# Attention over 416 of 512 key columns, with tokens kept by grid columns from the second norm to the output

## The reference

```python
h = _rmsnorm(x, pre_g[i]) * (1.0 + sc[:, None, :]) + sh[:, None, :]
hc = _rmsnorm(ctx, pre_g[i]) * (1.0 + sc_c) + sh_c
parts = _split_in(h @ w_in[i])
q = _apply_rope(_heads(parts[4]), cos, sin)
k = _apply_rope(_heads(parts[5]), cos, sin)
...
attn = _neighbourhood_attention(q, k, v, k_c, v_c, rpb[i])
y = _mixer_out(parts, attn, conv_w[i], conv_b[i], w_out_conv[i], w_out_attn[i], w_o[i])
...
x = x + gt[:, None, :] * _rmsnorm(y, post_g[i])
```

## Time and profile before

| | |
|---|---|
| time, 3 runs | 1209.0, 1209.19, 1211.04 us; median 1209.19 |
| profiled execution, its own time | 1211.35 us |
| its span | 1209.5 us |
| granted TensorE clock, mean | 0.991 |
| busy: PE, PEld | 1158.9 us (96%), 682.9 us (56%) |
| busy: DVE, ACT, POOL | 492.9, 239.3, 107.0 us |
| moved by DMA | 324.58 MB, mean 268 GB/s |

### The profile page before, as it was taken

One profiled execution on the slowest core, in us unless ns is written; L12 is line 12 of the kernel. 1 busy time (PEld: TensorE's weight loads), 2 busy tenths in 40 slices (PEclk: granted clock), 3 DMA queues, 4 the chain that ended last, 5 costly groups with the idle time before them and its releaser, 6 DMA issues.

```text
span 1209.5 us, 13265 instructions
## 1 busy us (share of the span) xinstructions
PE 1158.9 (96%) x5276; PEld 682.9 (56%) x5276; DVE 492.9 (41%) x832; ACT 239.3 (20%) x452; POOL 107.0 (9%) x116
## 2 busy tenths in 40 slices
PE   6999999999999999999989898899999999999997
PEld 6887888888344454453433243454447854456643
DVE  2146348424111201111111111276755676577677
ACT  2232554202100000000000000111001011038811
POOL 0016135000000000000000000000000020025300
PEclk9999999999999999999999999999999999999999
DMA  9999323377799999999999999954546446443300
GB/s 319 344 289 331 127 71 104 105 287 312 310 422 412 407 413 414 414 414 421 414 422 421 422 421 422 347 207 140 173 139 203 146 144 218 142 166 128 102 6 35
DMA packets 118999, 324.58 MB, mean 268 GB/s; under 512 B 8736, under 2 KB 66208, under 8 KB 94368
## 3 DMA queue, kind: packets, MB, share of 16 engines
q1 hardware_dynamic: 113200, 316.32, 68.9%
q0 software_dynamic: 1536, 4.20, 1.1%
q10 hardware_dynamic: 4208, 3.31, 0.9%
HBM read 322.75 MB, written 1.05 MB: 268 GB/s over the span
## 4 chain that ended last, share of the span: by engine, by line
PE 85%; DMA 9%; DVE 2%; ACT 1%; issue 1%; POOL 1%; SPq 0%; DVEq 0%; POOLq 0%
PE bank L719 21%; PE bank L698 17%; PE bank L1025 16%; DMA AR<-in_w 9%; PE bank L701 7%; PE bank L1066 7%; PE bank L1001 2%; PE bank L1037 2%; PE bank L1040 2%; PE bank L1173 1%; PE bank L1206 1%; PE bank L1186 1%; PE bank L1104 1%; PE bank L811 1%; PE bank L1052 1%
## 5 line engine op out<-in xcount | busy, mean ns | idle before, releaser
L698 PE MATMUL bank<-HT,ring 128*128 128x256 f32 x864 | 193.5, 382 | 0.0
L1025 PE MATMUL bank<-ring,AR 128*64 128x512 f32 x608 | 172.6, 610 | 16.0 <-DMA AR<-in_w 10.7
L698 PEld LDWEIGHTS bank<-HT,ring 128*128 128x128 f32 x864 | 163.2, 191 | 27.4 <-issue 6.5
L1025 PE MATMUL bank<-AR 128*64 128x512 f32 x416 | 125.8, 605 | 2.7 <-DMA AR<-in_w 2.6
L2117 DVE TENSOR_TENSOR AR<-AR,bank 128x256 f32<-128x256 f32 x32 | 13.5, 421 | 273.8 <-ACT AR L1427 273.1
L1025 PEld LDWEIGHTS bank<-ring,AR 128*64 128x64 f32 x608 | 50.5, 139 | 106.7 <-issue 103.7
L719 PE MATMUL bank<-ring,AR 128*128 128x512 f32 x224 | 99.8, 604 | 2.1 <-DVE AR L1778 1.1
L719 PE MATMUL bank<-ring,HN 128*128 128x512 f32 x224 | 97.3, 592 | 0.0
L1066 PE MATMUL bank<-ring,AR 128*64 128x512 f32 x352 | 79.6, 594 | 0.0
L719 PEld LDWEIGHTS bank<-ring,AR 128*128 128x128 f32 x224 | 42.8, 194 | 56.0 <-issue 54.0
L719 PE MATMUL bank<-ring,HT 128*128 128x512 f32 x168 | 73.7, 593 | 0.0
(11 more groups left out here) (353 smaller groups left out, 1376.6 us busy)
## 6 DMA issues: line engine op xcount, KB each, us to landing
ring<-in_w SPq DMA_DIRECT2D x120, 1024.0 KB, 17.2
AR<-in_w SPq DMA_DIRECT2D x72, 1024.0 KB, 15.0
ring<-in_w_in SPq DMA_DIRECT2D x61, 1024.0 KB, 7.0
ring<-in_w_mod SPq DMA_DIRECT2D x12, 1024.0 KB, 9.0
AR<-in_w_in SPq DMA_DIRECT2D x6, 1024.0 KB, 18.1
ring<-in_w_out SPq DMA_DIRECT2D x4, 1024.0 KB, 5.4
ring<-in_w_ple_gate SPq DMA_DIRECT2D x4, 1024.0 KB, 9.3
AR<-in_bias POOLq DMA_DIRECT2D x32, 128.0 KB, 2.4
```

Of the source, the lines that this page charges most:

```text
L698: mm = pe.matmul(bank[:, part * T:part * T + T], w[:, k, c0 + part * P:c0 + part * P + P], act[:, k, :], start=(k == 0), stop=(k == k_n - 1))
L1025: mm = pe.matmul(bank[e * SLOT:e * SLOT + SLOT, :].rearrange("p (w n) -> p w n", w=2), XG[:, k, :], w, start=(k == 0), stop=(k == DK - 1))
```

## The change

The tokens behind the second norm are kept in another order: groups of 8 grid columns, all 4 rows of such a group together, so 32 tokens to a group, and tile 0 of the queries holds columns 0 to 31, tile 1 columns 32 to 63. The keys in `KK` lie as tile 0 (128), context (256), tile 1 (128). A window of 16 columns from tile 0 reaches no further than column 39, so tile 0 meets the first 416 entries and tile 1 the last 416 (`met(t)`). Scores, maximum, exponential and scaling run over 416; the other 96 weights are zeroed once on DVE, and turns and values stay at their size.

To get into this order `HT` is written permuted. The convolution needs row order: the turns of `conv` write their bank permuted back, and the last step of `conv_chunk` returns to the new order. ACT moves the context's keys from `KC` into `KK` in five copies. The bias table is permuted on the host, each bias tile is written in two pieces of 128 columns, and the window mask becomes 512 columns wide, so the constants grow by 256 columns. SP copies the input rows from X to `XC` in the new order, in 32 transfers of 8 partitions (32 KB each) inside the core, and stores each half of the output with four transfers of 32 partitions (64 KB) in place of one.

```diff
+BY_COLUMNS = np.arange(T).reshape(T // GW, GW // 8, 8).transpose(1, 0, 2).reshape(-1)
+NEAR = P + 32
...
-                  ("winmask", 256), ("invfreq", 16), ("iota_slot", 128), ("rev8", 8), ("pick2", 2), ("row0", 128), ("round_id", ROUNDS)):
+                  ("winmask", 2 * T), ("invfreq", 16), ("iota_slot", 128), ("rev8", 8), ("pick2", 2), ("row0", 128), ("round_id", ROUNDS)):
...
-        KK = area(1024, 2, DK, T)
-        KT2 = KK[:, 1]
+        KK = area(1024, DK, 2 * T)
+        KT2 = KK.rearrange("p k (b q) -> p k b q", b=4)[:, :, 0:4:3, :]
+        SHK = area(21520, 2, 512)
...
+        XC = area(E0 + 8192, TT, D)
...
+        def met(t):
+
+            return slice(t * (T - NEAR), t * (T - NEAR) + T + NEAR)
...
+        def grid_rows(v):
+
+            return v.rearrange("p (g r c) -> p r g c", r=T // GW, c=8)
...
+            sp.wait_ge(S("na_nmax"), H2 * TT)
+            for g in range(GW // 8):
+                for r in range(T // GW):
+                    n, m = g * 32 + r * 8, r * GW + g * 8
+                    sp.dma_start(XC[n % P:n % P + 8, n // P, :], X[m % P:m % P + 8, m // P, :]).then_inc(S("xrow_in"), 16)
+            rows = out[0].rearrange("(r g c) d -> g r c d", r=T // GW, c=8)
...
-                    sp.dma_start(out[0, t * P:t * P + P, c], HN[:, t, c]).then_inc(S("stored"), 16)
-            sp.wait_ge(S("stored"), 16 * TT * 2)
+                    for g in range(4):
+                        sp.dma_start(rows[4 * t + g, :, :, c], HN[32 * g:32 * g + 32, t, c]).then_inc(S("stored"), 16)
+            sp.wait_ge(S("stored"), 16 * TT * 2 * 4)
...
+                        dst = dst.rearrange("p (r g c) -> p g r c", r=T // GW, c=8)
...
-                    pe.matmul(B[2 + 2 * (u % 2) + e][:, :].rearrange("p (s t) -> p s t", s=2),
-                              QT2[p0:p0 + HD, c, t * P:t * P + P], KK[p0:p0 + HD, :, c, :], start=True, stop=True)\
-                      .then_inc(S("na_s"), 1)
+                    pe.matmul(B[2 + 2 * (u % 2) + e][:, met(t)], QT2[p0:p0 + HD, c, t * P:t * P + P],
+                              KK[p0:p0 + HD, c, met(t)], start=True, stop=True).then_inc(S("na_s"), 1)
...
-                nc.scalar.activation(HT[:, k, :], B[4 + k // 2][:, (k % 2) * T:(k % 2) * T + T], ACT.Identity,
+                nc.scalar.activation(grid_rows(HT[:, k, :]), B[4 + k // 2][:, (k % 2) * T:(k % 2) * T + T]
+                                     .rearrange("p (r g c) -> p r g c", r=T // GW, c=8), ACT.Identity,
...
+            for c0, n in ((4, 4), (2, 2), (1, 1)):
+                if c0 < 4:
+                    act.wait_ge(S("cT"), DK + 3 - c0)
+                nc.scalar.activation(KK[:, c0:c0 + n, P:P + T], KC[:, c0:c0 + n, :], ACT.Copy).then_inc(S("cT"), 1)
+            nc.scalar.activation(YA[:, 0, :], KC[:, 0, :], ACT.Copy).then_inc(S("cT"), 1)
+            act.wait_ge(S("cT"), DK + 4)
+            nc.scalar.activation(KK[:, 0, P:P + T], YA[:, 0, :], ACT.Copy).then_inc(S("cT"), 1)
...
+                pr = PR2[:, n % 4, met(n // 2 % 2)]
+                nc.scalar.activation(pr, pr, ACT.Exp, scale=-1.0, bias=NMX2[:, n % 4:n % 4 + 1],
...
-                        V_.tensor_scalar(HT[:, k, :], src, gain(k), bias(k), ALU.mult, ALU.add).then_inc(S(done), 1)
+                        V_.tensor_scalar(grid_rows(HT[:, k, :]), src.rearrange("p (r g c) -> p r g c", r=T // GW, c=8), gain(k),
+                                         bias(k), ALU.mult, ALU.add).then_inc(S(done), 1)
...
+                m = met(n // 2 % 2)
+                V_.tensor_tensor_reduce(PR2[:, n % 4, m], B[2 + n % 4][:, m], BM[:, n % 4, m], -1.0, 3e38,
...
+                    V_.memset(PR2[:, 0:2, T + NEAR:2 * T], 0.0)
+                    V_.memset(PR2[:, 2:4, 0:T - NEAR], 0.0)
                     na_max(0)
...
+                dve.wait_ge(S("xrow_in"), 16 * (1 + T // 8))
+                V_.scalar_tensor_tensor(out=HN[:, t, c], in0=YF[:, t, c], scalar=rs["y"][:, t:t + 1], in1=XC[:, t, c],
```

More of the change, by code:

```diff
@@ L82, in constants @@
     inv = 10000.0 ** (-np.arange(0, half, 2, dtype=np.float32) / np.float32(half))
-    t = np.arange(T)
+    t = BY_COLUMNS
     d = np.arange(P) % HD
@@ L89, in constants @@
     put("sinT", np.sin(ang.astype(np.float64)) * np.where(i % 32 < 16, -1.0, 1.0)[:, None])
[L90 to L94, removed]
+    col = BY_COLUMNS % GW
+    for tile in range(2):
+        qc, kc = col[tile * P:tile * P + P], col
+        start = np.clip(qc - WIN // 2, 0, GW - WIN)
+        inside = (kc[None, :] >= start[:, None]) & (kc[None, :] < start[:, None] + WIN)
+        at = CONST_COLS["winmask"][0] + tile * T
+        c[:, at:at + T] = np.where(inside, 0.0, -1e30)
     put("invfreq", 10000.0 ** (-np.arange(16, dtype=np.float32) / np.float32(16)))
@@ L1139, in turn_quarter @@
                 for k in range(4):
-                    mm = pe.transpose(TURN_BANKS[name][n][:, k * P:k * P + P], quarter_rows(name, n)[:, k * P:k * P + P], ident)
+                    dst = TURN_BANKS[name][n][:, k * P:k * P + P]
+                    if name == "conv":
+                        dst = dst.rearrange("p (r g c) -> p g r c", r=T // GW, c=8)
+                    mm = pe.transpose(dst, quarter_rows(name, n)[:, k * P:k * P + P], ident)
                 mm.then_inc(S("mT_ps"), 1)
@@ L1182, in values2 @@
                 for kt in range(4):
-                    v = VC if kt < 2 else V2
+                    v = (V2[:, 0], VC[:, 0], VC[:, 1], V2[:, 1])[kt]
                     for e in range(2):
                         h = 2 * c + e
-                        mm = pe.matmul(B[0][e * HD:e * HD + HD, 0:T], v[:, kt % 2, h * HD:h * HD + HD],
+                        mm = pe.matmul(B[0][e * HD:e * HD + HD, 0:T], v[:, h * HD:h * HD + HD],
                                        turned2(c, e)[:, kt, :], start=(kt == 0), stop=(kt == 3))
@@ L1491, in rows_turned @@
                 t, half, _ = QUARTERS[n]
-                dst = {"gated": YA, "conv": UC[:, :, 1:T + 1], "merged": MT}[name]
+                dst = {"gated": YA, "conv": UC[:, :, 1:T + 1], "merged": MT}[name][:, 4 * half:4 * half + 4, :]
                 act.wait_ge(S("mT_ps"), quarter_count(name, n))
-                nc.scalar.activation(dst[:, 4 * half:4 * half + 4, t * P:t * P + P],
-                                     TURN_BANKS[name][n][:, :].rearrange("p (k q) -> p k q", k=4), ACT.Copy)\
-                  .then_inc(S("mT"), 1)
+                if name != "conv":
+                    dst, src = dst[:, :, t * P:t * P + P], TURN_BANKS[name][n][:, :].rearrange("p (k q) -> p k q", k=4)
+                else:
+                    dst = dst.rearrange("p k (r t q) -> p k r t q", r=T // GW, t=TT)[:, :, :, t, :]
+                    src = TURN_BANKS[name][n][:, :].rearrange("p (k r q) -> p k r q", k=4, r=T // GW)
+                nc.scalar.activation(dst, src, ACT.Copy).then_inc(S("mT"), 1)
             first_copy("za")
@@ L1684, in _ @@
                 pool.wait_ge(S(f"bt{n % 4}"), 16 * (n // 4 + 1))
-                bm = BM[:, n % 4, T:2 * T]
-                nc.gpsimd.tensor_tensor(bm, bm, const("winmask"), ALU.add).then_inc(S("bm"), 1)
+                mask = const("winmask").rearrange("p (t b k) -> p t b k", t=TT, b=2)[:, n // 2 % 2]
+                nc.gpsimd.tensor_tensor(bias_at(n), bias_at(n), mask, ALU.add).then_inc(S("bm"), 1)
                 if n >= 2 and n + 2 < H2 * TT:
@@ L2214, in conv_chunk @@
                                              op0=ALU.mult, op1=ALU.add))
-                return V_.tensor_tensor(YA[:, k, :], YA[:, k, :], cv, ALU.mult)
+                ya = grid_rows(YA[:, k, :])
+                return V_.tensor_tensor(ya, ya, cv.rearrange("p (r g c) -> p r g c", r=T // GW, c=8), ALU.mult)
             for m in range(8):
-                s = 1.0 if m >= 4 else HD ** -0.5
-                dst = two(QT2 if m < 4 else KT2, m % 4)
+                s = HD ** -0.5
+                dst = two(QT2, m) if m < 4 else SHK[:, m % 2, :]
                 i = (of["q2"] + of["k2"])[m]
```

22 lines of the change are left out of this document (13 added, 9 removed).

## The result

The changed kernel takes 1213.88 us (median of 6 runs, 1212.19 to 1215.34) beside 1209.39 us for the kernel before (6 runs, 1208.03 to 1211.62). The ratio is 1.0029, 95% interval 1.0019 to 1.0039: slower, by 3.5 us of 1209 (2.3 to 4.7). The forecast was +2.6 us. The change does both of the things that the prediction weighed, a gain in the attention and a loss at the stores.

What follows compares the result with a forecast made beforehand. TensorE, busy 1158.9 of 1209.5 us, bounds the kernel until its end, which hangs on the last store. Scores -2.4, exponential -0.2, stores +5.2 make +2.6 on 1209.19: 1211.8 us, own range 1210.2 to 1212.7, wide range 1207.4 to 1213.6.

Steps and rivals of the forecast that it cites:

- The scores: Attention's score steps on TensorE: 416 columns for 512 save 0.16 us a step, 2.4 us over 15 steps (1.8 to 3.0).
- The constant part of a step: In a score step's 1.06 us on TensorE, 0.20 us does not go with the columns and 0.86 does.
- rival 4: Attention's odd steps: waits for ACT lose half of the 2.4 us, with four store engines 1213.0 us; 0.14 together with rival 3.
- The slack of about 0.3 us in the odd steps: Second head's turns need a bank that ACT empties: 0.36 us to spare, 0.29 left after the change.
- The stores: Kernel's end: sixteen transfers in line on the same four engines, 0.68 us each, 10.9 us; 5.2 us more (4.4 to 5.5).
- the term for an issue: SP's queue at the end: 0.33 us an issue, 0.38 us from one to the next.
- Rival 1: SP's queue at the end: stores spread over all sixteen engines, end costs 1.4 us, 1208.0 us in all; chance 0.22.
- What was taken at nothing: Row copies, ACT's key copies, permuted `HT` writes, conv's turns, longer constants, smaller bias transfers, DVE's fillings: counted as 0 us.
- the cover: Input-row copies on SP: in by about 1160 us, DVE first needs them at 1201.24; holds up to 1.7 us a copy.
- rival 3: Turns of conv on TensorE: they double, +1.75 us, with four store engines 1213.6 us; chance 0.14 together with rival 4.

Runs made afterwards that it cites:

- the four shapes: The kernel before, each output half stored in four transfers, of 2 by 16, 4 by 8, 8 by 4, 16 by 2 rows: 1215.02 us, one time.

## Why the prediction came out right, and where it was off

**The scores.** Forecast 0.16 us a step, 2.4 in all, and 0.2 for ACT's exponential: measured 0.16 a step, 0.08 for the exponential in the chain, and 2.55 together. The constant part of a step that the working assumed fits: without it the step would have lost 0.20. The kernel with 512 keys in the new layout shows the same from the other side: its middle is 2.56 us longer, and its ratio 0.17% higher (2.1 us) than the changed kernel's.

**No wait for ACT in its place** (rival 4). The slack of about 0.3 us in the odd steps held: the turns there went from 1.02 to 1.03 us, and no piece on ACT came into the chain in between.

**The stores.** Forecast 5.2 us (4.4 to 5.5): measured 5.45 in the two profiles, 5.6 between the ratios. The mechanism forecast, four engines and the same four each time, is what the packets, the share of 0.26 and the run with two queues show. But two steps of the working failed. First, the reason I gave from the row, that an engine gets eight rows whatever the size, is wrong: in the kernel before with 32-row stores an engine gets two rows, and only the rule on the slowest dimension, which I had set beside it, fits all of these kernels. By my reason stores of 32 plain rows would have cost 5 us as well; measured, they cost 2.1. Second, the term for an issue, 0.33 us and 0.38 from one to the next, was mis-sized: it is 0.616 and 0.66, nearly the 0.68 I took for moving 64 KB. With a single queue the issues keep almost the pace of the transfers, so the forecast's size was right for one of two limits that nearly coincide, and that they coincide was not foreseen. The run with two queues shows that the four engines alone hold the end at this length. That the issues alone would hold it within about 0.5 us is the estimate under the four shapes.

**Rival 1's price** was mis-sized by the same term. Spread over sixteen engines, stores of 32 plain rows cost 2.1 us and not 1.4, with issues of 0.42 us, one every 0.46. For the stores of the change, whose issues take 0.62, rival 1 would have come out near the forecast itself and not at 1208.0 us. The time alone could then not have told the two apart; the tiny packets, the share of 0.26 and the second queue do.

**What was taken at nothing.** The 32 copies took 21.5 us of SP and not 12, at 0.62 us an issue; they were in by about 1164 and DVE first wanted them at 1196.68, so the cover held. DVE's four writes of `HT` in runs of eight took 1.90 us, not the 2.9 that the working allowed for. The strided writes of `HT`, the turns of conv (rival 3), ACT's copies and the cut bias transfers together cost TensorE 377.88 - 377.88 = 0.00 us behind the norm. The longer constants lie in front of it, and the ratio of the kernel with 512 keys is the best witness for them: 5.6 us (4.1 to 7.1) against 5.4 for its end. That leaves no sign of a price, but would not show one of 0.4 us.

**The number.** 1211.8 us was 1209.19 + 2.6. The ratio applied to the same 1209.19 gives 1212.7, 0.9 above the forecast and inside the range. (The forecast's own range began at 1210.2; its terms, 0.63 us a transfer and 0.20 a step, add up to 1210.4.) The median of the changed kernel's six runs, 1213.88, stands 0.3 above the top of the range. Of the 0.9, 0.25 is the end; the rest is within the ratio's interval (1211.5 to 1213.9).

## What to carry to other kernels

Before splitting or permuting a transfer, look at the slowest dimension of each side: in all kernels here it set how many DMA engines carried it, and the tiny packets in the DMA view count them. Look at the number and the length of the issues beside it, since either can be the limit. A reordering of data is worth choosing by the transfer it ends in: two orders with the same 416 keys differed by 5.2 us in the traces (0.57% between the ratios), because one ends in sixteen stores of 4 by 8 rows and the other in four of 32 by 4. And where a saving sits in the middle of a kernel, time the stretch to the end of the last product and the tail behind it apart; the scatter of everything ahead of them hides both.

## What the runs showed of the hardware that was not expected

- An issue on SP depends on the shape: 0.33 us for 128 plain rows, 0.42 for 32 plain rows, 0.57 to 0.63 (medians) where the destination has a dimension more, whether that reached 2 or 16 engines (the first of a kernel took up to 0.82). The copies inside the core took 0.62 with plain rows (8 by 4 KB); why is open.
- Two queues (SP's and ACT's) with transfers of slowest dimension 4 held a share of 0.27 together: they use the same four engines and do not add up.
- TensorE's turns that write their bank in runs of eight elements, or in single elements 16 bytes apart, took the same 1.75 us for sixteen as plain ones. DVE and ACT wrote in runs of eight at no cost (1.90 and 1.93 us for four). Single elements took them a quarter more or a little over (2.39 and 2.50).
- The 32 copies inside the core, of 8 rows each, fit the count of engines by tiny packets as well: the view from 1140 to 1170 us of the changed kernel has 272, which are 16 for the last weights and 8 for each copy.
